# ScalarE makes a lot's diagonals right behind its gelu, and TensorE takes the lot's sums at the end of the same step

## The reference

```python
def block(xt):
    ...
    eidx = e1 * PEER_N_KEYS + e2
    g = jax.nn.softmax(sc, axis=-1)
    act = jax.nn.gelu(jnp.einsum('thkd,td->thk', expert_u[eidx], xt), approximate=False)
    w = (g * act.astype(jnp.float32)).astype(expert_v.dtype)
    return jnp.einsum('thk,thkd->td', w, expert_v[eidx])
```

## Time and profile before

| | us |
|---|---|
| median of 3 runs (4513.41 to 4517.97) | 4517.83 |
| the profiled execution | 4516.97 |
| its span in the profile | 4515.2 |
| PE busy / DVE busy / POOL busy / ACT busy | 3340.2 / 2758.0 / 1455.5 / 1212.7 |
| mean granted TensorE clock | 0.841 |
| DMA, the gathers' queue | 1142.47 MB |

### The profile page before, as it was taken

The page is one execution under the profiler, slowest core; times in us unless marked ns, Lnnn a source line. Parts: engine busy times, 40 slices in busy tenths (PEclk is TensorE's granted clock), DMA queues, the critical chain, the costliest instruction groups (busy, mean ns, idle before and its releaser), DMA issues.

```text
span 4515.2 us, 32805 instructions
## 1 busy us (share of the span) xinstructions
PE 3340.2 (74%) x10062; PEld 1694.6 (38%) x10062; DVE 2758.0 (61%) x5414; ACT 1212.7 (27%) x2631; POOL 1455.5 (32%) x1213
## 2 busy tenths in 40 slices
PE   6799997739894688789458888865767678645564
PEld 4344443524452244436124444532433334312221
DVE  1200001167559887757988784799767666996665
ACT  1111101225310355411136551111545421110110
POOL 0111001013222344333434442443323334444553
PEclk9999998767897788889779889987887789877787
DMA  3122111449986799999899999988888799979997
GB/s 124 55 77 93 63 67 35 173 163 363 358 303 233 288 411 398 372 378 386 327 347 398 395 372 366 392 345 328 329 314 334 282 374 378 385 296 376 420 420 283
DMA packets 251084, 1331.91 MB, mean 295 GB/s; under 512 B 29880, under 2 KB 73144, under 8 KB 104448
## 3 DMA queue, kind: packets, MB, share of 16 engines
q0 software_dynamic: 163232, 1142.47, 63.7%
q1 hardware_dynamic: 87680, 187.35, 11.6%
HBM read 1294.07 MB, written 35.10 MB: 294 GB/s over the span
## 4 chain that ended last, share of the span: by engine, by line
DVE 25%; PE 24%; DMA 15%; ACT 7%; issue 7%; SPq 3%; POOL 1%; ACTq 0%; DVEq 0%; POOLq 0%
PE pv L869 11%; DMA uv<-expert_uv,rows_u 10%; DVE uv L1249 10%; PE pb L978 4%; SPq L700 3%; PE pb L951 3%; DVE held L1273 2%; PE pb L926 2%; DMA arena<-w_stream 2%; PE pb L851 2%; DMA arena<-out_sv_p 2%; PE pb L822 1%; POOL uv L776 1%; DMA uv<-expert_uv,rows_pk 1%; DVE arena L1319 1%
## 5 line engine op out<-in xcount | busy, mean ns | idle before, releaser
L776 POOL DMA_INDIRECT uv<-expert_uv,rows_u x1024 | 1319.9, 1289 | 2298.2 <-PE pv L869 1379.8
L869 PE MATMUL pv<-uv,diag 128*128 128x512 f32 x2640 | 1515.7, 732 | 721.8 <-ACT diag L1093 639.0
L1249 DVE CUSTOM_DVE_ANT_0 uv<-uv,nr 128x1024 f32<-128x1024 f32 x1056 | 1244.1, 1220 | 311.6 <-DMA uv<-expert_uv,rows_u 271.9
L869 PEld LDWEIGHTS pv<-uv,diag 128*128 128x128 f32 x2640 | 604.2, 238 | 1523.4 <-issue 1438.0
L248 PE MATMUL ps<-win,xg 128*128 128x512 f32 (+1 forms) x1440 | 630.6, 596 | 0.0
L1100 ACT ACTIVATE gel<-dots 128x4 f32<-128x4 f32 x264 | 54.2, 205 | 1885.6 <-DVE dots L1249 1885.5
L1273 DVE SCALAR_TENSOR_TENSOR held<-uv,wgt,held 128x1024 f32<-128x1024 f32 x387 | 497.3, 1285 | 13.7 <-DVE wgt L1260 0.3
L822 PE MATMUL pb<-arena 64*128 64x512 f32 (+6 forms) x544 | 247.0, 564 | 197.7 <-DMA arena<-out_sv_p 118.9
L248 PEld LDWEIGHTS ps<-win,xg 128*128 128x128 f32 (+1 forms) x1440 | 260.9, 184 | 342.8 <-issue 342.5
L372 DVE TENSOR_SCALAR ffz<-ffz 128x72 f32<-128x72 f32 x1 | 0.2, 198 | 502.6 <-ACT ffa L314 502.6
L851 PEld LDWEIGHTS pb<-arena 128*128 128x128 f32 (+3 forms) x1728 | 210.9, 181 | 95.7 <-issue 64.7
(11 more groups left out here) (163 smaller groups left out, 2612.6 us busy)
## 6 DMA issues: line engine op xcount, KB each, us to landing
arena<-w_stream SPq DMA_DIRECT2D x80, 1024.0 KB
win<-w_main SPq DMA_DIRECT2D x10, 2048.0 KB, 8.8
uv<-expert_uv,rows_u POOLq DMA_INDIRECT x1024
scratch_gates<-stage POOLq DMA_DIRECT2D x32, 256.0 KB, 2.3
arena<-scratch_gates SPq DMA_DIRECT2D x8, 1024.0 KB, 20.5
xg<-x_t SPq DMA_DIRECT2D x8, 536.0 KB, 7.5
arena<-scratch_c_p SPq DMA_DIRECT2D x8, 520.0 KB
xr<-x SPq DMA_DIRECT2D x8, 512.0 KB, 4.3
```

The source lines that it names most:

```text
L776: pool.indirect_dma_start(out=uv[k % NU][:].rearrange("p a n -> p (a n)"), out_offset=None, in_=io["expert_uv"][:, :], in_offset=bass.Indi ...
L869: mm = nc.tensor.matmul(pv[:, c * BANK:(c + 1) * BANK], diag[n % ND][:], uv[k % NU][:, 1, c * BANK:(c + 1) * BANK], start=n == first, stop ...
L1249: nc.vector.tensor_tensor_reduce(out=u, in0=u, in1=row[:], scale=1.0, scalar=0.0, op0=ALU.mult, op1=ALU.add, accum_out=dots[b % 2][:, k % ...
```

## The change

ACT makes the diagonals of lot b directly behind gelu b, in both parts of a wave and in the tail (`ahead` and `behind` become one `beside`); PE sums lot b, not b - 1, at the end of the step that has lot b. `close` moves to the first lot of the next tile. No instruction is added or taken away apart from how they group; line numbers behind the edit shift by one or two.

```diff
@@ -880,8 +880,7 @@
 
                 def beside(step):
                     for b in plan.lots.get(step, ()):
-                        if b:
-                            background(b - 1)
+                        background(b)
 
                 def attend(g):
                     n0, units = plan.first[g], plan.end[g] - plan.first[g]
@@ -1020,8 +1019,7 @@
                     attend(g)
                     merge(g)
                 for b in plan.rest:
-                    background(b - 1)
-                background(plan.rest[-1])
+                    background(b)
                 fold()
 
             @block.scalar
@@ -1099,16 +1097,10 @@
                         act.wait_ge(weighted, b - 1)
                     nc.scalar.activation(gel[b % 2][:], dots[b % 2][:], ACT.Gelu).then_inc(gelu, 1)
 
-                def ahead(step):
-                    for b in list(plan.lots.get(step, ()))[:1]:
-                        if b:
-                            diagonals(b - 1)
-
-                def behind(step):
-                    for i, b in enumerate(plan.lots.get(step, ())):
-                        if i:
-                            diagonals(b - 1)
+                def beside(step):
+                    for b in plan.lots.get(step, ()):
                         gelus(b)
+                        diagonals(b)
 
                 def attend(g):
                     n0, units = plan.first[g], plan.end[g] - plan.first[g]
@@ -1121,11 +1113,10 @@
                             turn_out(n0 + s - 1)
                         if inside:
                             probabilities(n0 + s)
-                            ahead(("attend", g, s))
                         if s >= 2:
                             take_output(n0 + s - 2)
                         if inside:
-                            behind(("attend", g, s))
+                            beside(("attend", g, s))
                             if plan.lots.get(("attend", g, s), ()):
                                 nc.scalar.preload_act_table_set("natural_log_exp_and_others")
 
@@ -1174,7 +1165,6 @@
                                              ACT.Copy).then_inc(q_out, 1)
 
                     for s, step in enumerate(merge_steps(tiles)):
-                        ahead(("merge", g, s))
                         if step[0] == "outputs":
                             take_outputs()
                         elif step[0] == "merged":
@@ -1190,15 +1180,14 @@
                             r = query_rows(t)
                             act.wait_ge(shifted, t + 1)
                             nc.scalar.activation(ex[0:r], ex[0:r], ACT.Exp).then_inc(expd, 1)
-                        behind(("merge", g, s))
+                        beside(("merge", g, s))
 
                 for g in range(len(WAVES)):
                     attend(g)
                     merge(g)
                 for b in plan.rest:
-                    diagonals(b - 1)
                     gelus(b)
-                diagonals(plan.rest[-1])
+                    diagonals(b)
 
             @block.vector
             def _(dve):
@@ -1259,7 +1248,7 @@
                         dve.wait_ge(summed, dve_slots[(b - 1) * LOT])
                     nc.vector.tensor_tensor(w[:], gel[b % 2][:], lot_gates(b), ALU.mult).then_inc(weighted, 1)
                     dve.wait_ge(weighted, b + 1)
-                    if b * LOT - t * NK == LOT and t:
+                    if b * LOT == t * NK and t:
                         close(t - 1)
                     for k in range(b * LOT, (b + 1) * LOT):
                         if not plan.on_dve(k):
```

## The result

| us | before | changed kernel |
|---|---|---|
| median | 4517.9 (4513.41 to 4521.27, 4 runs) | 4936.07 (4931.73 to 4942.59, 4 runs) |
| span of the profiled execution | 4515.2 | 4935.3 |
| mean granted TensorE clock | 0.841 | 0.815 |

The account below looks back on a forecast made before the run. Bounds taken: DMA (0.98, 0.97 busy) in attention of waves 2 and 3, PE in wave 2's merge, mutual waits in wave 4's attention, transfers in the tail. Attention 173 + merges 156 - close 46 = +283 on 4516.97, forecast 4800 us, range 4620 to 4920.

Parts of the forecast that it names:

- part 1: Attention of all waves: ACT and PE wait for the present lot, so steps grow; 173 us slower in all.
- The loop through PE's queue: Wave 3 attention: PE's wait, sums, values, transposes and ACT's work up to the next gelu close a loop of 12.6 us.
- The 1.0 us for ACT's own diagonals in the long step: Wave 3 attention: ACT's wait for the weighing plus its diagonals lengthen the long step to 14.4 us, called certain.
- Part 1, wave 1: Wave 1 attention, a lot at every second step: same loop gained, 1.9 us for each of 16 lots, 30 us slower.
- Part 2: Merges of all waves: PE stands waiting for the present lot in projection and query steps; 156 us slower in all.
- Wave 1's merge: Merge of wave 1, with half the lots: 20 us slower, against 48 for wave 2's merge.
- The steps behind the queries: Pick and expert steps after the merges' queries: nothing on PE but the sums, so they cost nothing.
- Part 3: Tile boundaries and tail: moving close gains 46 us, 16 in the tail and 5 at each of six boundaries inside waves.
- (a): Whole kernel: release wins, PE and ACT have slack and gathers start a step earlier; 4380 us, chance 0.07.
- (b): Whole kernel: nothing moves, transfers cover the chains and the boundaries return the merges' loss; 4510 to 4526 us, chance 0.04.
- (c): Only one of attention and merges gets slower: 4644 us for attention alone, 4627 for merges alone, chance 0.22.
- (d): Sums behind a wait run at 1.2 GHz: +270 us, 5070 at the extreme, 4920 or more if half; chance 0.12.

Follow-up runs that it names:

- run 2: Kernel before with only ACT's diagonals moved right behind their own lot's gelu, PE still one lot late, 5 diagonal buffers: 4523.3 us, ratio 1.001.
- Run 7: Changed kernel with wave 1 in the old order and the tail's close late: 4817.4 us, ratio 1.0659 to the kernel before.
- run 10: Kernel before with ACT's early diagonals and PE waiting for the present lot's diagonals at step end, after summing the lot before: 4646.5 us, ratio 1.0294.
- run 1: Kernel before with only close moved to the next tile's first lot: 4474.6 us, ratio 0.9905.
- runs 3 and 4: Kernel before with the changed order in the attention steps alone, then in the merge steps alone: 4707.1 us (1.042) and 4746.4 us (1.0504).
- runs 8 and 9: Changed kernel, tail's close late, with 10, then 4, added matmuls of zeros before PE's wait for diagonals in attention: 4928.1 and 4924.5 us.

## Why the prediction was right and wrong

- **What bounds the kernel, and part 1's mechanism: right for waves 2 to 4.** The loop through PE's queue exists, with 11.9 and 14.6 us where 12.6 and 14.4 were worked out, in the half of wave 3 where the three-slot lots fall on the long step (13.8 and 15.3 in the other half); stages +43, +64, +34 against 45, 58, 40. The 1.0 us for ACT's own diagonals in the long step is there in size (10 us in wave 3 for 16) though I called it certain, and it doesn't add up over the kernel (+0.1% in run 2).
- **Part 1, wave 1: the step that failed.** "Its lot step gains the same loop and the step without one hides little: 1.9 us for each of 16 lots, 30 us." Measured is 66 us, 4.1 a lot over the stage and 5.7 from lot 7 to lot 14. The first lots, at 2.9, are not far from the forecast; the failure is in the others. The loop is not the same there: with a free step between two lots, and the lots on the steps that begin with magnitudes, these stand behind the copy that waits for PE, and PE's sums and DVE's dots come one after the other. I had read the order of the queues for one step and carried its result over to a stage in which the next lot is two steps away. Run 7 shows the size of wave 1's share, and run 10, with this stage at 201.7 us for 202.0, that the place of the sums costs it and not the wait; the series itself is read from the rows above and was not tested by itself.
- **Part 2: right for waves 2 to 4** (+51, +53, +46 for 48, 48, 40; 6.39 us for 6.5 behind a projection). **Wave 1's merge was mis-sized**, 61 for 20, by taking half the lots for less than half the cost. In its first part before (columns as in the earlier trace rows)

```profile
1192.00:1376.00 184.00, 167.98 (x591) 106.02 (x590) 92.62 (x268) 29.25 (x58) 43.40 (x34) 0.93 0.83 316
```

  PE was busy 168 of 184 us, at a clock of 0.93, so it had little slack to hide a wait. Of the 61 us, 27 are the wait's (run 10), and in the changed kernel PE stands there (1257 to 1517 us; in total, times, longest)

```profile
PE pv L869 <- ACT diag L1091: 55.3, 9, 10.3
```

  The rest goes with the sums, which follow each wait at a lower clock: 0.83 over this window. That split is from run 10; that the clock is what the rest lost in this stage was not tested.
- **The steps behind the queries: not nothing.** I wrote that they cost nothing; they and the next wave's first steps took 21 us more. I have no experiment on these steps alone. Together they took 626.6 us before, 647.4 in the changed kernel, 642.6 with attention alone, 629.1 with merges alone and 635.3 with the early close alone, so most of it comes with the attention's order and the close; how is open.
- **Part 3: right by itself, only half of it in the changed kernel.** 46 us forecast, 40 measured alone (run 1). In the changed kernel the tail gained its 16 us, but PE still waits 76.6 us for the closing rows where it waited 81.8, so the 30 us for the boundaries inside the waves are not shown there.
- **Where the error comes from.** The time passed the forecast by 136 us. By the stage table some 77 of them are wave 1's (127 for 50), 21 the steps behind the queries, 12 the other stages, and the 30 us taken off for the boundaries were not gained; that is 140, with the rounding of the stages in it. The good match of waves 2 to 4 is in part luck: half of wave 3's pairs took 29 us where 27 were forecast, and the later ones 27. Any of the three larger terms, put right, would have brought the time into the range, wave 1's to 4859 us.
- **Rivals.** (a) and (b) are refuted: DVE waited less for its rows, 99 us for 272, and it gave nothing. (c) is refuted by runs 3 and 4. (d), the clock: the measured 4936 us lie where I had put (d), at 4920 or more, but not for its reason. The sums' mean rose by 8%, not by half, runs 8 and 9 give back 24 to 28 us, and PE's busy time grew by 114 us in all, not by 270. The range was too low at the top because it left no room for wave 1's terms, which I had bounded at 2.4 us a lot.

## To carry to other kernels

Before making a consumer take its input one step earlier, write down what stands behind it in its queue and who waits for that: a lag of one step between two engines costs buffer time, but it is what keeps a slow producer out of the consumer's other work. If the lag varies over the program, work the loop out again for each spacing and for each kind of step on which the input falls; a result from one stage doesn't carry over. And test the small parts of a change by themselves: here the one line that moved `close` was worth 0.95% in the old order, while the rest cost nearly 10%.

## What I had not expected of the hardware

Halving the sums' instructions (2640 to 1338) took their busy time only from 1516 to 1007 us, while the granted clock fell from 0.841 to 0.767 and the median of one instruction rose from 592 to 1061 ns: part of the time saved by removing work came back as slower instructions. And work added in a wait made the work behind it faster (789 to 702 ns an instruction with ten matmuls of zeros ahead, at a clock of 0.864 for 0.815), but the 211 us that the sums lost stand against 545 us of added work.
